# MLP down projection on one Trainium2 core: seven block products in place of eight, with sums of hidden blocks and two sets of weight sums

## The reference, cut to what matters

```python
D_MODEL = 1024; SEQ = 512; D_FF = 4 * D_MODEL; DEPTH_2 = 2

def mlp_sq_relu(h, w1, w2):
    return jnp.square(jax.nn.relu(h @ w1)) @ w2

# in second_block, for i in range(DEPTH_2):
#   y = rms_norm_2(h, norm1[i]); y = mixer_a(...) or mixer_b(...)
#   h = h + y
#   h = h + mlp_sq_relu(rms_norm_2(h, norm2[i]), mlp_w1[i], mlp_w2[i])
```

## Time and profile before

| what | value |
|---|---|
| device time, median of 3 runs | 2930.82 us (2929.42 to 2931.16) |
| span of the profiled execution, first to last instruction | 2930.3 us |
| execution of that profile as timed from outside | not given apart; the median is 0.5 us above its span |
| PE busy | 2753.7 us, 94% of the span |
| DVE busy | 1123.4 us, 38% |
| ACT busy | 916.9 us, 31% |
| POOL busy | 781.5 us, 27% |
| granted TensorE clock, mean | 0.990 of full speed |
| stretch of the first MLP | 2040.3 to 2389 us |
| stretch of the second MLP | 2578 to 2926 us |

### The profile page before, as it was taken

One profiled execution on the slowest core, in us unless ns is written; L12 is line 12 of the kernel. 1 busy time (PEld: TensorE's weight loads), 2 busy tenths in 40 slices (PEclk: granted clock), 3 DMA queues, 4 the chain that ended last, 5 costly groups with the idle time before them and its releaser, 6 DMA issues. The chain is left out here.

```text
span 2930.3 us, 51243 instructions
## 1 busy us (share of the span) xinstructions
PE 2753.7 (94%) x22943; PEld 2152.7 (73%) x22943; DVE 1123.4 (38%) x1554; ACT 916.9 (31%) x1458; POOL 781.5 (27%) x216
## 2 busy tenths in 40 slices
PE   7999989888989998888999999989999999999999
PEld 5877878778774333334899989987888888888887
DVE  5435765664552111114543475353211124431111
ACT  4133242343351000002355445543322232242222
POOL 2321332132120000001322332312444434434443
PEclk9999999999999999999999999999999999999999
DMA  7112201103165999996312221221332323322331
GB/s 276 53 33 63 65 4 63 62 3 106 48 244 223 424 426 427 427 427 257 128 58 73 72 86 54 78 72 58 101 101 88 99 87 101 99 88 89 100 101 58
DMA packets 171436, 397.00 MB, mean 135 GB/s; under 512 B 9519, under 2 KB 99604, under 8 KB 145876
## 3 DMA queue, kind: packets, MB, share of 16 engines
q1 hardware_dynamic: 170240, 390.34, 36.4%
q10 hardware_dynamic: 980, 3.40, 0.3%
HBM read 387.36 MB, written 4.19 MB: 134 GB/s over the span
## 5 line engine op out<-in xcount | busy, mean ns | idle before, releaser
L186 POOL TENSOR_TENSOR weight_ring_lo<-weight_ring,weight_hi 128x2048 fp32r<-128x2048 f32 (+1 forms) x144 | 656.9, 4562 | 1788.2 <-ACT weight_hi L175 1745.4
L175 ACT CAST weight_hi<-weight_ring 128x2048 fp32r<-128x2048 f32 (+1 forms) x144 | 271.4, 1886 | 550.1 <-PE late L244 309.9
L244 PE MATMUL late<-weight_hi,latT_hi 128*128 128x512 f32 x572 | 175.3, 429 | 0.0
L225 PE MATMUL late<-latT_lo,weight_hi 128*128 128x512 f32 x680 | 167.9, 389 | 0.0
L225 PE MATMUL late<-latT_hi,weight_ring_lo 128*128 128x512 f32 x680 | 167.9, 389 | 0.0
L225 PE MATMUL late<-latT_hi,weight_hi 128*128 128x512 f32 x680 | 167.9, 389 | 0.0
L244 PE MATMUL late<-weight_ring_lo,latT_hi 128*128 128x512 f32 x572 | 156.6, 396 | 0.0
L244 PE MATMUL late<-weight_hi,latT_lo 128*128 128x512 f32 x572 | 155.8, 394 | 0.0
L225 PEld LDWEIGHTS late<-latT_hi,weight_ring_lo 128*128 128x128 f32 x680 | 127.6, 188 | 26.5
L225 PEld LDWEIGHTS late<-latT_lo,weight_hi 128*128 128x128 f32 x680 | 127.6, 188 | 26.5
L225 PEld LDWEIGHTS late<-latT_hi,weight_hi 128*128 128x128 f32 x680 | 127.6, 188 | 26.5
(11 more groups left out here) (696 smaller groups left out, 5226.8 us busy)
## 6 DMA issues: line engine op xcount, KB each, us to landing
weight_ring<-in_mlp_w SPq DMA_DIRECT2D x64, 1024.0 KB, 5.3
weight_ring<-in_w_gate SPq DMA_DIRECT2D x41, 1024.0 KB, 15.2
weight_ring<-in_w_down SPq DMA_DIRECT2D x38, 1024.0 KB, 15.2
weight_ring<-in_w_up SPq DMA_DIRECT2D x36, 1024.0 KB, 12.7
weight_ring<-in_a_wqkv SPq DMA_DIRECT2D x36, 1024.0 KB, 5.0
weight_ring<-in_w_mod SPq DMA_DIRECT2D x24, 1024.0 KB, 5.7
weight_hi_spare<-in_w_up SPq DMA_DIRECT2D x16, 1024.0 KB, 12.5
weight_hi_spare<-in_w_down SPq DMA_DIRECT2D x16, 1024.0 KB, 15.1
```

The costliest lines, as they stand in the source:

```text
L175: self.nc.scalar.copy(self.view(self.hi[:, q % 2], p, True), self.view(self.slots[self.slot[p]], p, True)).then_inc(self.hi_ready, 1)
L186: self.nc.gpsimd.tensor_tensor(self.view(self.lo[:, s], p, True), self.view(self.slots[s], p, True), self.view(self.hi[:, q % 2], p, True) ...
L225: last = nc.tensor.matmul(dst, left(a, k), right(b, k), start=(a + b + k == 0), stop=(a == 1 and k == KD - 1))
L244: last = nc.tensor.matmul(dst, left(a, HK * r + k), right(b, k), start=(r + a + b + k == 0), stop=(r == 1 and a == 1 and k == HK - 1))
```

## The change

The down projection is no longer done as plain block products. For each pair of up panels (512 hidden columns) the 512x512 hidden block and its 512x1024 piece of `w2` are each seen as 2x2 blocks, and Winograd's form of Strassen's scheme needs seven products of a token half (256 tokens) with 256 rows by 512 columns, where the plain way needs eight. A product is 12 matmuls (two token tiles, two row blocks, three passes), so a pair costs 84 in place of 96. The partial sums stay in PSUM: two chains of two banks each (`chain` in `SEVEN`), to which product after product is added, while DVE adds the running bank to `x` after each product (`drain`).

The scheme needs four sums of hidden blocks (`combine`, each with one operand in PSUM) and four sums of weight blocks (`form_seven`, three in the new buffer `own`, one in place; `own` has two sets). The stream now has items beside panels: a down pair is seven items of 128x1024, taken from the two loaded panels and from `own`, each of which is rounded by ACT and reduced by POOL on its own. `weight_hi` is now four units of 128x1024; an up panel takes two neighbouring units (so it may have to skip one), an item one. POOL reduces an up panel as two halves of 128x1024, with one semaphore at the end.

The order is now: two up panels, then in turn two up panels and the seven products of the pair before. The hidden blocks of an odd up panel (`hidden_at`) are rounded and lowered only in the turn of the following even one, except in the first two panels and in the last.

```diff
+    def add_item(self, split, shape, raw, lo, panel=None, formed=0, settled=0, halves=False):
...
+            n = -(-shape[0] * shape[1] // HI_UNIT)
+            self.hi_at += -self.hi_at % n
+            units = [(self.hi_at + i) % HI_UNITS for i in range(n)]
+            self.hi_at = (self.hi_at + n) % HI_UNITS
+            item.hi = units[0] * HI_UNIT
+            item.hi_before = max(self.hi_holder[i] for i in units)
...
+    def add_seven(self, w, rows, turn):
...
+        self.add_item(True, shape, raw(0, 0), low(0, 0), panel=pair[0], settled=t1)
+        self.add_item(True, shape, raw(0, 1), low(0, 1), panel=pair[0], settled=t4)
+        self.add_item(True, shape, *own(3 * turn + 1), formed=t2, settled=t4)
+        self.add_item(True, shape, *own(3 * turn), formed=t1, settled=t2)
+        self.add_item(True, shape, raw(1, 0), low(1, 0), formed=t3, settled=t3)
+        self.add_item(True, shape, raw(1, 1), low(1, 1), panel=pair[1], settled=t2)
+        self.add_item(True, shape, *own(3 * turn + 2), formed=t4, settled=t4)
...
+    def form_seven(self, dve, group):
...
+        V.tensor_tensor(t1, b12, b11, ALU.subtract).then_inc(self.formed, 1)
+        V.tensor_tensor(b12, b22, b12, ALU.subtract).then_inc(self.formed, 1)
+        dve.wait_ge(self.formed, group.n + 1)
+        V.tensor_tensor(t2, b22, t1, ALU.subtract).then_inc(self.formed, 1)
+        dve.wait_ge(self.formed, group.n + 3)
+        V.tensor_tensor(t4, b21, t2, ALU.subtract).then_inc(self.formed, 1)
...
+    def round_next(self, act):
+
+        item = self.items[self.split[self.rounded]]
+        w = item.shape[2]
+        if item.formed:
+            act.wait_ge(self.formed, item.formed)
+        else:
+            act.wait_ge(self.full[self.slot[item.panel]], self.landed[item.panel])
+        if item.hi_before >= 0:
+            act.wait_ge(self.used, item.hi_before + 1)
+        self.nc.scalar.copy(self.hi_view(item)[:, :, 0:w], item.raw()[:, :, 0:w]).then_inc(self.hi_ready, 1)
...
+    def round_behind(self, act, n, stop):
+
+        while self.rounded < len(self.split) and self.split[self.rounded] < stop and self.items[self.split[self.rounded]].hi_before < n:
+            self.round_next(act)
...
     def reduce_until(self, pool, n):
...
+            if item.settled:
+                pool.wait_ge(self.formed, item.settled)
             pool.wait_ge(self.hi_ready, q + 1)
...
+            n_part = 2 if item.halves else 1
+            for i in range(n_part):
...
+            last.then_inc(self.lo_ready, 1)
...
+HI_UNIT = KD * PW // 2
+HI_UNITS = 4
...
+N_UP = FF // PW
+N_DOWN = N_UP // 2
+SEVEN = ((0, 0, 0, 0), (1, 1, 0, 0), (4, 0, 0, 1), (3, 1, 1, 1), (5, 0, 1, 1), (6, 1, 0, 1), (2, 0, 1, 0))
+FRESH = (0, 1, 3)
...
 def mlp_order():
...
+    order = [("up", 0), ("up", 1)]
+    for n in range(N_DOWN):
+        order += [("up", u) for u in (2 * n + 2, 2 * n + 3) if u < N_UP] + [("down", n)]
     return order
...
+        hidden_at = lambda n: [n] if n < 2 else [n - 1, n] if n % 2 == 0 and n > 2 else [n] if n == 2 else []
...
         @block.tensor
         def _(pe):
...
+                if kind == "up":
+                    w = st.take_split(pe)
+                    if n >= 2:
+                        pe.wait_ge(up_free, n - 1)
...
+                pe.wait_ge(hidden, 2 * n + 2)
+                for i, (block_of, chain, _, _) in enumerate(SEVEN):
+                    w = st.take_split(pe)
+                    for s in range(2):
+                        if i >= 2:
+                            pe.wait_ge(drained, 14 * n + 2 * (i - 2) + s + 1)
+                        elif n:
+                            pe.wait_ge(drained, 14 * (n - 1) + 2 * (6, 5)[i] + s + 1)
+                        for a, b in ((0, 0), (0, 1), (1, 0)):
+                            for k in range(2):
...
         @block.scalar
...
+            for t, (kind, n) in enumerate(order):
+                if kind == "up":
+                    act.wait_ge(st.used, at[t] + 1)
+                    relu(n)
+                    st.round_behind(act, at[t] + 1, stop)
+                    for u in hidden_at(n):
+                        round_own(u)
+                        round_sums(u)
                     continue
+                for i in range(len(SEVEN)):
+                    act.wait_ge(st.used, at[t] + i + 1)
+                    st.round_behind(act, at[t] + i + 1, stop)
+                    if n + 2 == N_DOWN and i == 0:
+                        round_own(N_UP - 1)
+                        round_sums(N_UP - 1)
...
         @block.vector
...
+            def lower(u):
+                dve.wait_ge(own_rounded, u + 1)
+                V.tensor_tensor(hid_parts[1][:, u % 4, 0], from_up(u, 0)[:, 0], hid_hi[:, u % 4, 0].bitcast(F32), ALU.subtract)
+                V.tensor_tensor(hid_parts[1][:, u % 4, 1:3], from_up(u, 1), hid_hi[:, u % 4, 1:3].bitcast(F32), ALU.subtract).then_inc(up_free, 1)
+                dve.wait_ge(sums_rounded, u + 1)
+                V.tensor_tensor(hid_parts[1][:, u % 4, 3:7], hid[:, u % 4, 3:7], hid_hi[:, u % 4, 3:7].bitcast(F32), ALU.subtract).then_inc(hidden, 1)
...
+            for t, (kind, n) in enumerate(order):
+                if kind == "up":
+                    hide = hidden_at(n)
+                    for u in hide:
+                        square(u)
+                        combine(u)
+                        if u == n and n % 2 == 0 and n:
+                            st.form_seven(dve, groups[n // 2 - 1])
+                        lower(u)
+                    continue
+                for i in range(len(SEVEN)):
+                    for s in range(2):
+                        drain(n, t, i, s)
...
+                    if n + 2 == N_DOWN:
+                        if i == 0:
+                            square(N_UP - 1)
+                            combine(N_UP - 1)
+                        elif i == 1:
+                            lower(N_UP - 1)
+                        elif i == 2:
+                            st.form_seven(dve, groups[n + 1])
```

283 lines of the change are left out of this document (152 added, 131 removed).

## The result

| | median | lowest to highest | runs |
|---|---|---|---|
| before | 2930.24 us | 2929.42 to 2931.16 | 4 |
| changed | 3083.59 us | 3079.26 to 3086.76 | 4 |

The changed kernel is slower by a ratio of 1.0514 (95% interval 1.0497 to 1.0531), 153 us. The forecast was 3050 us, the range 3005 to 3090. Direction, places and most sizes held; the increase came out 34 us larger than forecast.

The account below looks back on a forecast made before the run. PE's own work and its new waits were taken to bound both MLPs. From 2930.3 us, -43.5 + 61 + 52 + 18 + 1 + 31 = +119.5 gave 3049.8, with 0.5 for the median 3050 us; range 3005 to 3090.

Parts of the forecast that it names:

- wait 1: Before odd up panels 5 to 15, PE waits for PSUM banks freed late by lowering: 12 x 5.1 = 61 us.
- wait 2: Before even up panels 4 to 14, PE waits for rounding and POOL behind the sixth product: 12 x 4.3 = 52 us.
- 192 matmuls: In both MLPs, PE saves 192 matmuls of 0.2267 us at full value: -43.5 us.
- seventh groups: DVE's four weight sums stand ahead of adds PE needs: 9 us per MLP, 18 us, between 8 and 23.
- clock behind the waits: PE at half clock after 26 MLP waits: 0 to 1.7 us each, 1.2 taken, 31 us.
- third item: At the products' start, its remainder comes slightly after PE asks: 0 to 1 us per pair, 0 taken.
- the ends: After the MLPs, 0.5 us for the norm and 0.5 for two stores: 1 us.
- stages ahead of the MLPs: Stages outside the MLPs keep their instructions; no time was added for them.
- turns everywhere: DVE and POOL alternate in every pair: 2.4 us at 12 third items, seventh groups 11.6; 3084 us, chance 0.18.
- The covered rival: At the two new waits, chains are released early enough that PE stays dense: 2888 us, chance 0.06.

Follow-up runs that it names:

- Experiment 1: Changed kernel, but ACT rounds the odd panel's hidden blocks before it waits for the end of the even up panel: 3004.75 us, ratio 1.0252.
- experiment 2: Changed kernel, but PE starts an up panel on the rounded part and waits for POOL's remainder only before its third pass: 3014.83 us, ratio 1.0287.
- experiment 4b: Changed kernel with 16 and 20 small unused matmuls on PE before even and odd up panels, inside the two waits: 3041.90 us, ratio 1.0375.
- experiment 5: Changed kernel, but ACT no longer waits for the end of the very last product before the norm's squares: 3080.58 us, ratio 1.0505.
- experiment 6: Changed kernel with both early rounding of odd-panel hidden blocks and up panels started on their rounded part: 2942.82 us, ratio 1.0036.
- the best version: Changed kernel with early rounding, rounded passes first, spread weight sums, no last-product wait, weight casts before relu, adds before norm scaling: 2915.90 us, ratio 0.9936.

## Why the prediction was right in its mechanism and short in its size

The direction, the two waits, the stall and their places came as forecast, inside the range. The increase was forecast as 120 us and measured as 153, and most of the difference is one term, the clock.

| term | predicted | measured in the trace |
|---|---|---|
| 192 matmuls | -43.5 | -43.5 (the count and the 0.2267 us hold) |
| wait 1 | +61 | 12 x 5.13 = +61.6 |
| wait 2 | +52 | 12 x 4.33 = +52 |
| seventh groups | +18 | 2 x 8.8 = +17.7 |
| clock behind the waits | +31 | 30.1 behind wait 2, 20.2 behind wait 1, 3.0 behind the seventh stalls = +53.3 |
| third item | 0 | 2 x 0.5 = +1.0, in the first pair of each MLP |
| the ends | +1 | +6.2, the norm of the first MLP |
| stages ahead of the MLPs | 0 | +5.8 |
| sum | +119.5 | +154.1; the spans differ by 154.7 (3085.0 against 2930.3) |

**Wait 1, right.** Five steps of the chain came within 0.1 us of the rows of before: casts 1.99 for both (2 x 1.05 less overlap), 0.39 and 0.61, DVE 1.02. Experiment 1 removes it by moving ACT's rounding alone, with every operation kept. That shows the cause to be ACT's order and not its load. The cover that wait 1 gave the third item was seen rightly as well.

**Wait 2, right.** ACT's cast started at 2216.47, when the sixth product ended (2216.3), and POOL's two halves took 4.67 us behind it; experiment 2 hides POOL's part and takes the wait to 0.6 us. That the sixth item's unit is the one waited for is read from the start of the cast; no run gave the panel another unit, so the unit alone was not tested.

**The seventh group, right, by luck of a middle value in part.** I took 9 between 4.2 and 11.6; the trace has 8.2 idle and 0.6 around it (0.3 idle ahead of the fifth product, and twice 0.17 of lost overlap). The walk had the place and the releaser; the turn-taking came as the earlier trace rows had it, for three of the four sums. The rival "turns everywhere" gave 3084 us, next to the measured time, but not for its reason: its loss at the third item did not occur while PE was late, and the normal period is explained to 0.1 us without it. A total that fits is no proof of a mechanism.

**The clock, the step that failed in size.** The prediction's step was "So a wait costs between 0 and 1.7 us more, and I take 1.2". The upper bound came from one place in the attention stage, where 1.70 us were lost behind a break in PE's work, and I used it as the ceiling. In the MLPs the even panel behind wait 2 lost from 1.71 to 2.67 us (2.5 in the mean), above that bound in eleven of twelve places and at it in the other, and the odd one behind wait 1 lost 1.5 to 1.7, near the bound. So the term was 24 x 2.1 and 3.0 in place of 26 x 1.2, and 22 of the 34 us that were missing lie in it. A duration read once at one place was taken for a limit of the mechanism. Nor are 2.5 and 1.7 prices of these two waits: the longer wait lost less, and in experiment 2 the same wait of 4.87 us lost from 1.5 to 3.0 us. The Trainium skill (TensorE: Matmul & The Clock Gate, "HAM oscillation — how this bites in real kernels") has this case as its rule, and here the trace agrees with it more fully than I gave it credit for: every one of the 24 long waits was followed by matmuls at 1.2 GHz, and experiment 4b got 42 us back by work inside the waits.

**The ends.** I priced the last tiles of `x` as 1.36 us closer together plus a little DVE work, and overlooked that ACT waits for the end of the last product before it starts on squares. That is the kind of wait I had listed for the up panels, on the same engine, in the same loop. Without ACT's wait (experiment 5) 1.6 of the 6.2 us go, and 1.15 more would have gone but for DVE's turn behind POOL there, if the scaling sets the pace as it does here; that was not tested apart. Another 1.5 lie behind the start of the nine filler matmuls by the identity that the kernel keeps at this place (L334, 18 records), which ran at half clock, 4.05 us in place of 2.17: from there to the next stage 7.8 us passed in place of 6.3. The rest lies between the last product and the fillers, where no run takes it apart.

**The stages ahead of the MLPs** keep their instructions, and still the first MLP began 5.8 us later in the profiled execution. In the other runs' profiles it began between 2039.3 and 2047.2 us, without relation to the edits, and the half-clock time ahead of 2030 us varied from 58 to 82 us. So it may be the variation of single executions, as large as the term itself; what sets it is open.

**The covered rival** (2888 us, chance 0.06) fell. Its break-even point, waits under 1.8 us each, counted only the two waits against the saved matmuls: with both at or below 0.6 us (experiment 6) the kernel is still at 1.0036, the seventh groups, the small POOL waits and the norm making up the difference.

## What to carry to other kernels

Where fewer matmuls are bought with more buffers' hand-overs, walk each engine's program order once per period and ask which release stands behind a wait for something later. Here two such places cost 141 us together, and the fix moved no work from one engine to another. Price a new idle gap of PE as the gap and the slow matmuls behind it, and give the second a range and no ceiling from a single row: here gaps of 4 to 5 us were followed by 1.5 to 3.0 us of lost time, 2.1 in the mean. Then expect most of a small saving to stay in small waits: of 43.5 us, the best version kept 18.

## What the runs showed of the hardware that was not expected

- DVE operations with two SBUF inputs and POOL operations, both queued, took turns: a DVE sum of 1.22 us took 3.35 to 3.42 and a POOL remainder of 2.40 took 3.31 to 3.37, in the seventh group and in normal periods. The Trainium skill (SBUF — State Buffer, "Who interferes with whom") says that such a DVE instruction contends with POOL's reads over a shared pair of ports and calls the pair an exclusive lock. The trace agrees: each operation ended 1.1 us (DVE) or 2.2 us (POOL) behind the other engine's end. That the other comes next, though more of the first are queued, the rows here show.
- A DVE operation with one large SBUF input and one column of scalars was held up by POOL as well, at one place (experiment 5): 1.90 us in place of 0.75, ending 0.56 us behind POOL's operation, which took its usual 4.60 us. Adds with one input in PSUM took 0.69 beside POOL throughout.
- A float32 matmul of 128x128 by the identity makes two records and takes 0.23 us in a dense row of them (7.31 us for 32), at full clock. That is as long as a 128x512 matmul in the rounded format (0.2267 us).
- The waits of 0.5 to 0.6 us in otherwise dense work (24 in both MLPs) left the window's granted clock at 1.00 (experiment 4b). Waits of 4 to 5 us took it to 0.50 behind each of the 24 in the changed kernel, and the time lost was not in proportion to the wait: 2.62 us behind 4.17, 1.71 behind 4.96, and 1.5 to 3.0 behind the same 4.87 in experiment 2.
